# Taking the matmuls that nobody reads out of the routing of a two-layer mixture-of-experts trunk

## The reference, cut to what matters

```
gl = x @ w_group + b_group                  # 4 group logits per token
top_g = argmax(gl);  p_g = softmax(gl)[top_g]
el_g = (x @ w_router + b_router)[group top_g]   # 4 expert logits of that group
top_v, top_i = top_k(el_g, 2)
gates = one_hot(experts) * softmax(top_v) * p_g
y = sum over experts of ((silu(x @ w_gate) * (x @ w_up)) * gate) @ w_down
```

## Time and profile before

| what | value |
|---|---|
| median of 3 runs | 678.98 us (676.75 to 679.55) |
| profiled execution, its own time | 678.86 us |
| its span in the profile | 677.1 us |
| TensorE busy | 645.6 us, 95% of the span |
| VectorE, ScalarE, GpSimd busy | 31%, 22%, 4% |
| mean granted TensorE clock | 0.983 of full speed |
| DMA | 150.05 MB, mean 222 GB/s |

### The profile page before, as it was taken

How to read it: one execution, slowest core, us unless ns; L and a number is a source line. 1 busy time by engine, 2 the same in 40 slices (tenths; PEclk the granted TensorE clock), 3 DMA queues, 4 the chain that set the end, 5 groups by cost and what they waited for, 6 DMA issues and landing times.

```text
span 677.1 us, 7895 instructions
## 1 busy us (share of the span) xinstructions
PE 645.6 (95%) x3036; PEld 398.0 (59%) x3036; DVE 208.0 (31%) x600; ACT 146.8 (22%) x405; POOL 29.0 (4%) x60
## 2 busy tenths in 40 slices
PE   6889999999999999999988999999999999999994
PEld 3567786777676444455436777777766733334431
DVE  2233111222124543444443333433411441212201
ACT  1111112332031111111152333333302411111110
POOL 5000000000002000000001000000000110000000
PEclk9889899999999999999999999999999989999998
DMA  9997131012512899999997605020333379999931
GB/s 286 289 263 239 63 126 62 1 62 73 238 61 69 330 412 423 421 421 421 367 348 262 206 1 187 15 110 1 125 121 127 126 305 418 422 422 420 423 135 64
DMA packets 59114, 150.05 MB, mean 222 GB/s; under 512 B 10082, under 2 KB 42914, under 8 KB 46786
## 3 DMA queue, kind: packets, MB, share of 16 engines
q1 hardware_dynamic: 55554, 136.71, 53.8%
q0 software_dynamic: 2912, 10.64, 4.4%
q10 hardware_dynamic: 608, 2.16, 0.8%
HBM read 146.27 MB, written 3.23 MB: 221 GB/s over the span
## 4 chain that ended last, share of the span: by engine, by line
PE 91%; DVE 3%; ACT 3%; DMA 1%; issue 1%; SPq 0%; DVEq 0%; ACTq 0%; POOLq 0%
PE bank L1228 34%; PE bank L1473 17%; PE bank L1497 8%; PE bank L1512 5%; PE bank L1516 4%; PE bank L1323 3%; PE bank L1445 3%; PE bank L1391 2%; PE bank L1646 1%; PE bank L1633 1%; PE bank L1237 1%; PE bank L1255 1%; PE bank L1675 1%; PE bank L1359 1%; DMA qk_area<-xs,idx 1%
## 5 line engine op out<-in xcount | busy, mean ns | idle before, releaser
L1228 PE MATMUL bank<-xT,ring 128*128 128x272 f32 x640 | 158.6, 404 | 5.2 <-ACT qk_area L535 3.0
L1228 PEld LDWEIGHTS bank<-xT,ring 128*128 128x128 f32 x640 | 123.5, 196 | 33.1 <-issue 6.8
L1473 PE MATMUL bank<-ring,gate_area 128*64 128x512 f32 x512 | 116.9, 604 | 0.9 <-ACT gate_area L635 0.9
L1473 PEld LDWEIGHTS bank<-ring,gate_area 128*64 128x64 f32 x512 | 35.2, 138 | 70.2 <-issue 69.9
L1228 PE MATMUL bank<-tok,ring 128*128 128x272 f32 (+1 forms) x256 | 61.0, 391 | 0.6 <-DVE tok L1212 0.6
L1497 PE MATMUL bank<-ring,gate_area 128*64 128x512 f32 x256 | 57.7, 593 | 0.0
L1228 PEld LDWEIGHTS bank<-tok,ring 128*128 128x128 f32 x256 | 47.4, 190 | 13.5 <-issue 6.1
L1497 PEld LDWEIGHTS bank<-ring,gate_area 128*64 128x64 f32 x256 | 18.2, 137 | 36.5 <-issue 36.5
L959 DVE TENSOR_TENSOR qk_area<-qk_area,bank 128x256 f32<-128x256 f32 x16 | 6.7, 421 | 100.4 <-ACT qk_area L643 100.4
L468 POOL DMA_INDIRECT qk_area<-xs,idx x16 | 16.3, 1019 | 452.6 <-DVE idx L846 211.1
L643 ACT ACTIVATE qk_area<-bank 128x256 f32<-128x256 f32 x16 | 6.1, 384 | 128.2 <-PE bank L1473 128.2
(11 more groups left out here) (255 smaller groups left out, 616.7 us busy)
## 6 DMA issues: line engine op xcount, KB each, us to landing
ring<-in_moe_w_gate SPq DMA_DIRECT2D x32, 1024.0 KB, 11.3
ring<-in_moe_w_up SPq DMA_DIRECT2D x32, 1024.0 KB, 13.8
ring<-in_moe_w_down SPq DMA_DIRECT2D x32, 1024.0 KB, 18.5
ring<-in_m_w_in SPq DMA_DIRECT2D x12, 1024.0 KB, 11.2
ring<-in_kv_w SPq DMA_DIRECT2D x8, 1024.0 KB, 11.9
ring<-in_m_w_out SPq DMA_DIRECT2D x4, 1024.0 KB, 7.1
ring<-in_f_w_q SPq DMA_DIRECT2D x4, 1024.0 KB, 12.0
ring<-in_f_w_o SPq DMA_DIRECT2D x4, 1024.0 KB, 5.1
```

The source lines that it names most:

```text
L1228: ins = pe.matmul(bank[c % 2][:, 0:n], w[:, k, half * P:half * P + P], x[:, k, 0:n], start=(k == 0), stop=(k == KB - 1))
L1473: ins = pe.matmul(bank[1][s, :], xgT[b % 2][:, q, s], ring[:, r:r + 2, q * FE:(q + 1) * FE], start=(q == 0), stop=(q == KB - 1))
```

## The change

`keep_busy` and its five calls in `moe(l)` are gone. `moe` runs for both layers, so 52 float32 matmuls are gone in all. Everything else stands as it was.

```diff
                 pe.matmul(bank[2][:, 0:4 * NE], onesb[0:1, :], base4[0:1, :, :].rearrange("p t e -> p (t e)"), start=True,
                           stop=False, skip_group_check=True)
-                def keep_busy(n_):
-
-                    for _ in range(n_):
-                        pe.matmul(bank[3][:, 2 * P:4 * P], ones_f[:, :], iota_f[:, :], start=True, stop=True)
-
                 pe.wait_ge(*in_layer("lg_read", l, 1))
-                keep_busy(4)
                 pe.wait_ge(*in_layer("eall_ready", l, 1))
...
-                keep_busy(5)
                 if l == 0:
                     pe.wait_ge(*in_layer("xr_read", l, 1))
                 rows_of_slots(1, 0, (0,))
-                keep_busy(14)
...
                 rows_to_cols(0, 0)
-                keep_busy(2)
                 rows_to_cols(0, 1)
                 rows_of_slots(2, 1, (1,))
-                keep_busy(1)
                 for b in range(NPAIR):
                     gate_up(b)
```

## The result

| | before | changed |
|---|---|---|
| median of 11 runs each | 676.67 us | 682.96 us |
| lowest to highest | 675.30 to 679.55 | 681.37 to 685.88 |
| profiled execution, own time | 678.86 | 685.81 |
| its span | 677.1 | 684.0 |
| TensorE busy | 645.6 | 630.3 |

The ratio is 1.0089, with a 95% interval of 1.0069 to 1.0108: slower by 0.9%, about 6.0 us. The forecast was +6.2 us, reckoned from the profiled execution of 678.86 us, which is why it names 685.1; from the median of 676.67 it would be 682.9. Among all the runs of this document two executions, one of before at 1097.7 us and one of layer0_bare at 702.4, stood in a slow state at a lower clock, and the ratios leave them out.

What follows compares the result with a forecast made beforehand. TensorE, 91% of the span, was taken to bound the kernel. Layer 0 (−0.4 + 1.0 + 2.6 = +3.2) and layer 1 (−0.2 + 1.0 + 2.2 = +3.0) took 678.86 to 685.1 us; 8-in-10 range 681.2 to 689.5.

Steps and rivals of the forecast that it cites:

- The clock at gate_up(0): In both layers' routing, the granted clock falls to 0.50 in the wait and is at 1.2 GHz when gate_up(0) begins.
- The first group: Without keep_busy(4), the slot count starts 0.7 us earlier in layer 0; 0.4 us gained there after 0.3 for L1411.
- Layer 1's gather: Still released by the token rows' write to DRAM, so not earlier; 0.2 us gained at the first transpose after it.
- The transposes: Two groups of four gathered-row transposes before gate_up(0) run at half clock: 1.0 us more in each layer, bounds 0 and 1.1.
- gate_up(0): Its first work runs at half clock: 2.6 us lost in layer 0, 2.2 in layer 1.
- 3 to 6 us: Sign in the trace: clock at 0.50 in either layer until this long behind the first instruction of gate_up(0).
- The bound of 4.8: Upper bound in us for each layer's gate_up(0) loss, with all of it at the lower clock.
- B: Rival: low clock stays through gate_up(0) in one layer or comes back behind it; 689 us, chance 0.12.
- A: Rival: the clock is back quickly in gate_up(0), 1.2 us lost a layer; 681.7 us, chance 0.13.
- C: Rival: the clock does not fall in the routing, only gains of 0.9 us are left; 678.0 us, chance 0.05 with D.
- D: Rival: the change does not do what it says, fillers only on the path; sum as C's, chance 0.05 together with C.
- The sum of 695 us: Skill page's reading, set aside: whole throttled time priced, waiting included, 8 us a layer, about 695 us.

Runs made afterwards that it cites:

- layer0_bare: Against before, the unread matmuls are left out in layer 0 only and stay in layer 1; 680.67 us, ratio 1.0041.
- first_two: Against before, the first group of unread matmuls is cut from 4 to 2 in each layer; 677.54 us, ratio 1.0004.
- fewer: Against before, unread matmuls are 2, 3, 9, 1, 1 in place of 4, 5, 14, 2, 1 in each layer; 679.19 us, ratio 1.0027.
- transposes: Against before, each unread matmul is replaced by three unread 128x128 transposes; 677.29 us, ratio 0.9996.
- thin: Against before, all 52 unread matmuls stay but read one row of either operand instead of 128; 701.48 us, ratio 1.0325.

## Why the prediction was right

- **The clock at gate_up(0).** Right. It was to be at 0.50 at 208 to 212 and at 530 to 535; it was, in layer 1 from 531 on.
- **The first group.** 0.7 us earlier in layer 0: measured from the ranks, L1396 starts at 0.35 us for 1.09. The price of L1411 at half clock was set at 0.3 and is 0.04 us (0.57 for 0.53), so the gather starts 0.7 us earlier in relation to the ranks and not 0.4. There was little more to be had there: the write of the token rows lands at 204.98 in the chain of the changed kernel, 0.1 us behind the index (204.87), and the profile names it as the gather's releaser. The earliest start in any run is first_two's, 0.8 us earlier.
- **Layer 1's gather.** Released by the write of the rows, as said. The 0.2 us to be gained at the transposes was not: their first matmul starts 9.16 us behind the ranks for 9.20, since the gathered rows were there 4.9 us after the issue of the gather, and at most 4.7 before.
- **The transposes.** 1.12 us a group for 0.71; up to the evacuation's start 1.15 for 0.75. From the first transpose to `gate_up(0)` it is 0.8 us more in layer 0 (4.30 for 3.49) and 0.9 in layer 1 (4.31 for 3.38) where 1.0 was put in, taken from an estimate with a poor row (the first transposes).
- **gate_up(0).** Layer 1: 2.2 forecast, 2.21 measured. Layer 0: 2.6 forecast, 3.61 measured, since the clock was down for 8.4 us behind gate_up's first matmul and I had taken 4 with 0.6 us of loss on top. This is the term that was mis-sized. The price of half a microsecond for each microsecond of dense work at the lower clock was right: 8.4 us less 1.1 of one-column matmuls, halved, is 3.6, and 4.9 less 0.4 is 2.2 in layer 1. What was wrong is how long the clock stays down once work has resumed; the sign "3 to 6 us" failed in layer 0. The bound of 4.8 was worked out wrongly as well: it is half of the 9.5 us of `gate_up(0)`, while all of it at the lower clock would cost about 7.5, from the rows of the changed kernel (four times 1.74 for L1465, 0.4 for the transposes, 0.1 for L1405). The measured 3.61 lies under either.
- **The sum.** Layer 0 +3.7 for +3.2, layer 1 +3.1 for +3.0. In layer 0 the miss of 1.0 in `gate_up(0)` was half made up by the gather (0.3) and the transposes (0.2), which is luck. The two intervals together give +6.8 for a forecast of 6.2, and the medians 6.0 to 6.3; that these stand nearer to the forecast than the profiles do is luck too, within a spread of 4 us between executions.
- **The rivals.** B's stretch behind `gate_up(0)` came in the profile of the changed kernel at 558 us, just as before at 551, so it moved nothing. Its other half, `gate_up(0)` wholly at the lower clock, came for 8.4 of 13.2 us in layer 0, and was priced too low by the bound above. A, C and D did not happen. C was argued against with the wait of 1.75 us at 22 us; fewer and transposes kept the clock at 1.00 through waits of 2.1 to 2.7 us, though in layer 0 of fewer it fell 2 us after the wait. So the length of one wait alone doesn't decide it; before the fall at 22 us TensorE had been busy for only 2.35 of the 4 us from 18 to 22. The sum of 695 us worked out by the Trainium skill's page (TensorE: Matmul & The Clock Gate, "HAM oscillation — how this bites in real kernels") counts the waiting too and is ruled out: the clock was down for 20.5 us in layer 0 (203.3 to 223.8), and the layer lost 3.7.

One thing about the comparison: executions of either kernel differ by up to 4.5 us, and the profiles show where most of it may come from. Both profiled executions have a stretch at the lower clock at 22 us, far from the change; first_two's profile, whose span is only 672.9 us, has none there and none at 39 us, which is 3.4 of the 4.2 us between its span and that of before. Such stretches come and go with no change in the program up to there, so one pair of profiles is good for the terms and not for the total.

## What to carry to other kernels

Work that nobody reads can be worth its place when TensorE would otherwise be near idle for some microseconds ahead of dense float32 work: look at the granted clock at the first dense matmuls behind a wait, not at TensorE's busy share. Such fillers must do real work in the array (128 rows held the clock and one row didn't; nothing between was tried), must fit into the wait even if the clock falls, and none should stand in a gap that only just hides it. Taking part of them away can be worse than it looks, since those that are left then run at half speed and get onto the path.

## What the runs showed of the hardware that was not expected

- A TensorE that is busy all the time can lose its clock: one-row float32 matmuls back to back stood at 0.50 (thin, 201 to 216 us, with PE busy for 4.00 of 4.00 us in both stretches shown).
- Float32 transposes of 128 rows, 156 in place of the 52 unread matmuls, held the clock at 1.00 through the routing (202 to 210 us), across a wait of 2.05 us.
- At the lower clock, four float32 transposes took 1.12 us for 0.71, six one-column bf16 matmuls 0.57 for 0.53, and eight instructions of 512 columns 3.68 for 1.94. What hangs on the columns doubles, what is small hardly changes. Dense work lost half a microsecond for each microsecond at the lower clock (3.61 and 2.21 us in the two `gate_up(0)`).
